# One projection tile, its three kinds of product in another order

## The chip, the cores and the metric

The kernel runs on one core of a Trainium2 chip, as one launch. The metric is the device time of that launch in microseconds (us); the kernel before takes 1693.22 us (median of 3 runs, 1692.78 to 1693.87). Everything is float32 at the interface. The engines that matter here are TensorE (PE in the profile, with its weight loads as PEld), VectorE (DVE) and ScalarE (ACT).

## The reference

Two networks of two layers each, one behind the other. The first prepends 16 meta tokens to 256 tokens, so its activations have 272 columns in the kernel (`T1`); its second layer needs only 256 columns from the out projection on. The second runs on the 256 tokens and, in its first layer, on 256 context tokens beside them (512 columns, `T2`).

```python
# first network, both layers
hn = rms_norm(h, norm_mix_g[l]);  proj = hn @ w_in[l]           # 1024 -> 2560
...                                                             # differential attention, RG-LRU
h = h + jnp.concatenate([o_attn, o_rec], axis=-1) @ w_out[l]    # 1024 -> 1024
hn = rms_norm(h, norm_ffn_g[l])
g, u = jnp.split(hn @ w_gu[l], [D_FF], axis=-1)                 # 1024 -> 2 * 2816
h = h + (jax.nn.silu(g) * u) @ w_down[l]                        # 2816 -> 1024
# second network, both layers: mixer (gmlp and neighbourhood attention, then grouped attention)
f = conv_ffn(modulate(h, ...), w_up[layer], conv_w[layer], conv_b[layer], w_down[layer])
# conv_ffn: h = x @ w_up; 3-tap convolution over tokens; a, g = split; (silu(g) * a) @ w_down
```

Nearly all the arithmetic is in these projections. The down projection takes its input, the hidden rows, from what the up projection before it has just made: that pair occurs in every layer.

## The kernel before, in words

**Precision.** Each float32 operand is held as two parts in a shorter type: a high part and the low rest. A projection is then the sum of three products: high weights by high rows, high weights by low rows, low weights by high rows. Weights arrive by DMA in `raw`. ACT writes the high part to `WH_t` (`split_hi`, L2299, semaphore `w_hi`); DVE subtracts and writes the low part to `WL_t` (`split_lo`, L1572, semaphore `raw_done`, which stands for both parts being there). In the profile both are called `W_t`. The rows are `XH_t`/`XL_t` (normed activations) or, for a down projection, `AH_t`/`AL_t` (hidden rows).

**Tiles.** Weights stay in the array and activations stream. One output tile is 128 output rows by T columns (272, 256 or 512) in one of four banks of `PA`. With a contraction of 1024 there are 8 slices k of 128 and so 24 matmuls; a down projection is done in two halves of the hidden rows, 11 slices and 33 matmuls each. There are thus eight half down projections: two of 272 columns, two of 256, two of 512 and two of 256, in this order of time.

**Order on TensorE.** It is written out by hand. `linear_pe(L)` runs `body(i, s)` for each chunk s of a projection L, and in it each output tile `oo`. Per tile it waits for both parts of the weights (L894), for a free bank, and then goes through the slices. In the first tile of a projection only (`s == 0 and oo == 0`), it also waits, ahead of each slice k, for the rows of that slice: `L.ready(k)`. For normed rows that is `x_ready`, for a down projection it is `hid`, which DVE raises once it has written the low part of hidden slice k (L1618, `hidden_low`). A semaphore is thus raised when both the high and the low rows of a slice are there. Inside a slice the three products follow each other (L917).

**The end of an up projection.** Hidden slice 10 of a half comes from the last pair of up tiles. For the gated kind of the first network ACT and DVE take the two tiles out of PSUM and multiply them; ACT then splits a weight tile (L2299) and writes the high hidden row (L2379), and DVE splits the same weight tile (L1572) and writes the low hidden row (L1618). For the convolving kind of the second network there are the taps (L2457, L1695, L1703), the SiLU (L2469) and the product (L1723) before L2379 and L1618.

**Other paths.** The second tile of a down projection (`second_down`, L953 to L959) and the first four tiles of some projections (`four_tiles`, L977 and L1005) have their own code, which the change leaves alone: they take all products of high weights first, wait for `raw_done`, and then take those of low weights. `out_early` (L872) does half of the first out projection's slices ahead of time. `heads_amid(o, n)` puts a few small matmuls (`spread_heads`, L1449 and L1450, which wait for `m3_rows`) between the slices of two tiles of the last attention's projections; it is called with the slice's number n, at (tile 4, slice 5) and (tile 7, slice 6).

```python
if (o, n) == (4, 5):
    spread_heads(1)
elif (o, n) == (7, 6):
    pe.wait_ge(S("m3_ready"), 2)
    spread_heads(0)
```

Of the kernel before, what the change touches and what calls it, by code (L numbers as in the profile page):

```python
# [24 lines left out]
P = 128  # L25
# [12 lines left out]
RAW = 4  # L38
# [96 lines left out]
def program(nc, hT, ctxT, params, lamv, wgate, wsb, rpb, c_both, c_first, c_second,  # L135
            w_in1, w_out1, w_gu1, w_dn1, w_ada, w_in2, w_out2, w_qkv, w_outc, w_up2, w_dn2, out):
    ctx = ExitStack()
    with ctx:
# [5 lines left out]
        def S(name):  # L144

            if name not in sems:
                sems[name] = ctx.enter_context(nc.semaphore(name))
            return sems[name]
# [8 lines left out]
        WH_t, WL_t = W_t[:, W_at:W_at + 2 * CH], W_t[:, W_at + 2 * CH:W_at + 4 * CH]  # L157
# [195 lines left out]
        def linear(*a, **k):  # L353
            L = Linear(*a, **k)
            if lins:
                lins[-1].next, L.prev = L, lins[-1]
            lins.append(L)
            return L
# [120 lines left out]
        def tiles_ready(n, v=None):  # L479

            v = len(n.groups) - 1 if v is None else v
            return lambda k: ("x_ready", n.value("x_ready", k, v))
# [6 lines left out]
        def norm(writers, *a):  # L489

            n = Norm(*a, alone=not writers, own=0 if not writers else 3 if writers[-1].kt == KD else 1)
            for w in writers:
                w.stat = n
            if writers and isinstance(writers[-1], Linear):
                n.first, n.writer = writers[0], writers[-1]
            plan.append(("norm", n))
            return n

        writers = []
        for l in range(2):  # L500
            n = norm(writers, "pre", l, T1, H1, [(0, T1, ("mixg", l), None)])
# [22 lines left out]
            n = norm([first, rest], "pre", l, T, HV, [(0, T, ("ffng", l), None)])  # L524
# [5 lines left out]
        for l in range(2):  # L530
            both = [(0, SEQ, (l, 0, A_MIX), (0, 0)), (SEQ, T2, (l, 1, A_MIX), (0, 1))]
            T = T2 if l == 0 else SEQ
            if l == 0:
                n = norm(writers, "pre", l, T2, H2, both)
                second_start = n
                rdy = all_ready()
                w = linear("copy", w_in2, 4, T2, XV, None, dst=prj2, held=2, ada=2,
                           parts=[(0, SEQ, tiles_ready(n, 0)), (SEQ, T2, tiles_ready(n, 1))])
# [21 lines left out]
            w = linear("copy", w_out2 if l == 0 else w_outc, 4, T, XV, mixed, dst=YV)  # L560
# [178 lines left out]
        raw_done = [S(f"raw_done{i}") for i in range(RAW)]  # L739

        def repeat(eng, n, step, body, loop=True):

            groups = n // step if loop else 0
            if groups >= 2:
                with eng.Fori(0, groups) as i:
                    for s in range(step):
                        body(i, s)
            else:
                groups = 0
            for s in range(groups * step, n):  # L750
                body(0, s)

        def first(i, s, n):
            return isinstance(i, int) and s < n
# [70 lines left out]
        def _(pe):  # L825
# [14 lines left out]
            def ada_sums(slot, r):  # L840

                b, q = divmod(slot, 4)
                if q == 0:
                    ada_turn()
                    if b:

                        pe.wait_ge(S("ada_free") if b <= 6 else S("ada_row"), b)
                pe.wait_ge(raw_loaded[r % RAW], 16 * (r // RAW + 1))
                for k in (2 * q, 2 * q + 1):
                    for j in range(4):  # L850
                        c = j * 512 + k % 2 * 256
                        mm = pe.matmul(ada_psum[b // 6][0][32 * j:32 * j + 32, :], cpad[:, k, :], RAWV[:, r % RAW, c:c + 256],  # L852
                                       start=(k == 0), stop=(k == 7))
                mm.then_inc(raw_done[r % RAW], 2)
                if q == 3:
                    unturned.append(b)
# [18 lines left out]
            def linear_pe(L):  # L875
                if L.loop:

                    if L.a0:
                        pe.wait_ge(S("of_act"), L.a0)
                    if L.d0:  # L880
                        pe.wait_ge(S("of_dve"), L.d0)
                T, (hi, lo) = L.T, L.rhs

                def body(i, s):
                    for slot, r in L.inline(s):
                        ada_sums(slot, r)
                    if s == 0 and L.after:

                        pe.wait_ge(S(L.after[0]), L.after[1])
                    for oo in range(L.outs):  # L890
                        o = L.outs * s + oo
                        w = L.place(s, oo)

                        pe.wait_ge(raw_done[L.chunk(s, oo)[0] % RAW], L.split(i, s, oo))  # L894
                        if first(i, o, 4):
                            if L.prev and not L.loop and not L.early:

                                name, value = L.prev.evacuated(L.prev.n * L.prev.outs - 4 + o)
                                pe.wait_ge(S(name), value)
                        else:  # L900

                            if L.kind == "copy":
                                pe.wait_ge(S("of_act"), L.a0 + o - 3 + i * (L.outs * L.step))
                            elif L.kind in ("add", "conv"):
                                pe.wait_ge(S("of_dve"), L.d0 + o - 3 + i * (L.outs * L.step))
                            elif oo == 0:
                                pe.wait_ge(S("of_act"), L.a0 + s - 1 + i * L.step)
                            else:
                                pe.wait_ge(S("of_dve"), L.d0 + s - 1 + i * L.step)
                        for n, k in enumerate(L.order):  # L910
                            if s == 0 and oo == 0:

                                name, value = L.ready(k)
                                pe.wait_ge(S(name), value)
                            c = w + k * P
                            for m, (W, X) in enumerate(((WH_t, hi), (WH_t, lo), (WL_t, hi))):
                                mm = pe.matmul(PA[:, (L.b0 + o) % 4, 0:T], W[:, c:c + P], X[:, k, L.x0:L.x0 + T],  # L917
                                               start=(n == 0 and m == 0 and not L.early),
                                               stop=(n == len(L.order) - 1 and m == 2))
                            if L.beside and L.beside[0] == "heads":  # L920
                                heads_amid(L.beside[1] + o, n)
                        mm.then_inc(S("out_ready"), 1)
                        if L.beside:
                            {"gmlp": gmlp_pe, "heads": heads_pe, "first": first_pe}[L.beside[0]](L, L.beside[1] + o)
                    if L.lru and L.lru[1] + s == 3:
                        lru_gates(L.lru[0], 0)

                if L.kt == FH:
                    body(0, 0)
                    second_down(L)  # L930
                    for s in range(2, L.n):
                        body(0, s)
                    return
                if L.parts:
                    four_tiles(L)
                    for s in range(2, L.n):
                        body(0, s)
                    return
                repeat(pe, L.n, L.step, body, L.loop)
# [153 lines left out]
            def lru_gates(l, half):  # L1093

                if half == 0:
                    if l == 0:
                        keep_busy(PB[:, 3, :], 4)

                    pe.wait_ge(S("lr_xs"), l + 1)
                    pe.wait_ge(S("wg_lo"), l + 1)  # L1100
                    if l:

                        pe.wait_ge(S("ada_row"), 3)
                else:

                    pe.wait_ge(S("lr_sg"), 2 * l + 1)
                for i in (2 * half, 2 * half + 1):
                    for g in range(2):
                        w = slice((g * 4 + i) * P, (g * 4 + i + 1) * P)
                        for m, (W, X) in enumerate(((wgh_t, XCH), (wgh_t, XCL), (wgl_t, XCH))):  # L1110
                            mm = pe.matmul(PB[:, i % 2 * 2 + g, 0:T1], W[:, w], X[:, i, :],
                                           start=(m == 0), stop=(m == 2))
                mm.then_inc(S("lr_g"), 1)
# [340 lines left out]
            def heads_amid(o, n):  # L1454
# [8 lines that stand above are left out]
# [1531 lines left out]
```

## Time and profile before

| | |
|---|---|
| median of 3 runs | 1693.22 us (1692.78 to 1693.87) |
| profiled execution, its own time | 1691.35 us |
| its span | 1689.6 us |
| mean granted TensorE clock | 0.994 |
| PE busy | 1616.5 us, 96% |
| PEld busy | 1407.3 us, 83% |
| DVE busy | 1017.9 us, 60% |
| ACT busy | 870.0 us, 51% |
| matmuls, all | 11870 |
| matmuls of L917 | 7800 |

Busy shares say which engine is full on the average; the chain of waits says whose work followed whose up to the end; the timeline gives the start and length of runs of instructions. A matmul's own duration is longer than the distance from its start to the next one's, since they are pipelined: distances between starts are what a matmul costs.

### The profile page before, as it was taken

To read this page: it belongs to the slowest core of one execution; us is meant where nothing else is said; L and a number is where in the kernel's file an instruction comes from. 1 tells how busy PE (TensorE), PEld (TensorE's weight loads), DVE (VectorE), ACT (ScalarE), POOL (GpSimd) and SP (SyncE) were. 2 spreads that over 40 slices of the span, in tenths; PEclk is the share of its full clock that TensorE was granted. 3 is DMA by queue.
4 is the path that set the end of the run, shared out by engine and by line. 5 is a ranking of instruction groups with operands and counts; after the bars stand their busy time and mean duration, and the time that the engine had idled before them with its cause. 6 is when DMAs were issued, how large, how long until landed. Compare 5 with 4: busy or idle time off the path is not lost.

```text
span 1689.6 us, 28191 instructions
## 1 busy us (share of the span) xinstructions
PE 1616.5 (96%) x11870; PEld 1407.3 (83%) x11870; DVE 1017.9 (60%) x1577; ACT 870.0 (51%) x1467; POOL 21.1 (1%) x38
## 2 busy tenths in 40 slices
PE   6999999999999999999989999999999898999997
PEld 6968999989789999987648777888888674789997
DVE  7675545465856555724555764424555777687585
ACT  6764534448545344544564543323444547766563
POOL 0000000000000000300000000000000000000000
PEclk9999999999999999999999999999999999999998
DMA  7465445354556464772202452232213530164642
GB/s 298 145 245 210 160 157 202 135 191 143 200 187 240 152 233 145 220 222 75 75 1 73 177 200 101 86 125 100 84 53 125 200 125 26 52 224 154 233 146 92
DMA packets 60524, 253.94 MB, mean 150 GB/s; under 512 B 4976, under 2 KB 8304, under 8 KB 42480
## 3 DMA queue, kind: packets, MB, share of 16 engines
q1 hardware_dynamic: 59088, 249.01, 41.6%
q0 software_dynamic: 1312, 3.15, 1.0%
q8 instruction: 94, 1.54, 0.4%
q14 instruction: 30, 0.25, 0.0%
HBM read 251.09 MB, written 1.05 MB: 149 GB/s over the span
## 4 chain that ended last, share of the span: by engine, by line
PE 81%; DVE 10%; ACT 6%; issue 2%; DMA 0%; SPq 0%; DVEq 0%; ACTq 0%
PE PA L917 63%; PE PA L977 3%; DVE W_t L1572 2%; PE PB L1340 2%; PE PB L852 2%; PE PA L1005 2%; ACT W_t L2299 1%; PE PB L1327 1%; PE PA L954 1%; PE PA L959 1%; PE PA L953 1%; PE PA L872 1%; PE PB L1270 1%; ACT tmp L2742 1%; PE PA L1412 1%
## 5 line engine op out<-in xcount | busy, mean ns | idle before, releaser
L917 PE MATMUL PA<-XH_t,W_t 128*128 128x256 f32 (+2 forms) x3968 | 873.3, 314 | 4.1 <-DVE W_t L1572 1.8
L917 PEld LDWEIGHTS PA<-XH_t,W_t 128*128 128x128 f32 x3968 | 650.1, 188 | 59.8 <-issue 6.0
L1572 DVE TENSOR_TENSOR W_t<-raw,W_t 128x1024 fp32r<-128x1024 f32 (+1 forms) x344 | 445.0, 1298 | 306.1 <-ACT W_t L2299 305.7
L917 PE MATMUL PA<-XL_t,W_t 128*128 128x256 f32 (+2 forms) x1984 | 620.5, 313 | 0.0
L2299 ACT ACTIVATE W_t<-raw 128x1024 fp32r<-128x1024 f32 (+1 forms) x344 | 381.4, 1113 | 155.6 <-PE PA L917 136.5
L917 PEld LDWEIGHTS PA<-XL_t,W_t 128*128 128x128 f32 x1984 | 373.1, 188 | 23.2 <-issue 0.5
L917 PE MATMUL PA<-AH_t,W_t 128*128 128x256 f32 (+2 forms) x1232 | 266.1, 311 | 0.2
L917 PEld LDWEIGHTS PA<-AH_t,W_t 128*128 128x128 f32 x1232 | 201.2, 188 | 14.1 <-DVE AL_t L1618 0.8
L917 PE MATMUL PA<-AL_t,W_t 128*128 128x256 f32 (+2 forms) x616 | 190.7, 310 | 0.0
L2457 ACT ACTIVATE tmp<-PA,par 128x512 f32<-128x512 f32 (+1 forms) x88 | 58.4, 667 | 133.0 <-PE PA L917 125.3
L1695 DVE SCALAR_TENSOR_TENSOR tmp<-PA,par,tmp 128x510 f32<-128x510 f32 (+1 forms) x88 | 53.6, 613 | 120.5 <-ACT tmp L2457 119.6
L917 PEld LDWEIGHTS PA<-AL_t,W_t 128*128 128x128 f32 x616 | 116.1, 188 | 6.7
L2412 ACT ACTIVATE big<-PA 128x272 f32<-128x272 f32 (+2 forms) x68 | 31.7, 466 | 118.0 <-PE PA L917 107.2
L977 PE MATMUL PA<-XH_t,W_t 128*128 128x256 f32 (+1 forms) x288 | 47.0, 294 | 8.2 <-DVE XL_t L1768 5.1
L2742 ACT ACTIVATE tmp<-PA,small 128x512 f32<-128x512 f32 (+1 forms) x64 | 40.2, 639 | 26.0 <-DVE small L2161 26.0
L2161 DVE TENSOR_REDUCE small<-PA 128x1 f32<-128x512 f32 (+1 forms) x64 | 36.8, 618 | 27.1 <-PE PA L1526 13.0
L852 PE MATMUL PB<-raw,cpad_t 128*32 128x256 f32 x768 | 52.3, 391 | 0.5 <-DMA raw<-in_w_ada 0.4
L977 PEld LDWEIGHTS PA<-XH_t,W_t 128*128 128x128 f32 x288 | 39.5, 193 | 14.8 <-issue 9.6
L1703 DVE SCALAR_TENSOR_TENSOR tmp<-PA,par,tmp 128x510 f32<-128x510 f32 (+1 forms) x88 | 50.1, 608 | 0.3
L1327 PEld LDWEIGHTS PB<-cboth,tmp 128*128 128x128 f32 x224 | 24.2, 140 | 30.7 <-DVE tmp L2170 23.1
L2444 ACT ACTIVATE tmp<-PA 128x272 f32<-128x272 f32 (+1 forms) x44 | 17.1, 390 | 62.2 <-PE PA L917 55.4
L977 PE MATMUL PA<-XL_t,W_t 128*128 128x256 f32 (+1 forms) x288 | 45.1, 289 | 3.1 <-DVE XL_t L1821 3.0
(275 smaller groups left out, 1576.4 us busy)
## 6 DMA issues: line engine op xcount, KB each, us to landing
raw<-in_w_ada SPq DMA_DIRECT2D x48, 1024.0 KB, 5.1
raw<-in_w_gu SPq DMA_DIRECT2D x44, 1024.0 KB, 4.8
raw<-in_w_dn SPq DMA_DIRECT2D x64, 704.0 KB, 4.0
raw<-in_w_up SPq DMA_DIRECT2D x44, 1024.0 KB, 4.8
raw<-in_w_in SPq DMA_DIRECT2D x30, 1024.0 KB, 5.5
raw<-in_w_out SPq DMA_DIRECT2D x12, 1024.0 KB, 4.8
raw<-in_w_qkv SPq DMA_DIRECT2D x6, 1024.0 KB, 6.3
raw<-in_w_outc SPq DMA_DIRECT2D x4, 1024.0 KB, 4.8
```

The lines of the kernel that those rows point to most:

```text
L852: mm = pe.matmul(ada_psum[b // 6][0][32 * j:32 * j + 32, :], cpad[:, k, :], RAWV[:, r % RAW, c:c + 256], start=(k == 0), stop=(k == 7))
L917: mm = pe.matmul(PA[:, (L.b0 + o) % 4, 0:T], W[:, c:c + P], X[:, k, L.x0:L.x0 + T], start=(n == 0 and m == 0 and not L.early), stop=(n == ...
L977: pe.matmul(PA[:, bank % 4, a:b], WH_t[:, c:c + P], x[:, k, a:b], start=(k == 0 and x is hi), stop=False)
L1005: mm = pe.matmul(PA[:, bank % 4, a:b], WL_t[:, c:c + P], hi[:, k, a:b], start=False, stop=(k == KD - 1))
L1327: mm = pe.transpose(PB[:, 2 + c, kb * 128:(kb + 1) * 128], a_P[p % 3][c][:, kb * 128:(kb + 1) * 128], ident)
L1572: dve.tensor_tensor(WL_t[:, w:w + L.cols], RAWV[:, r % RAW, part * UNIT:part * UNIT + L.cols], WHf[:, w:w + L.cols], ALU.subtract).then_in ...
L1695: dve.scalar_tensor_tensor(c[:, :, 1:SEQ], ps[:, :, 0:SEQ - 1], tap(o, 0), c[:, :, 1:SEQ], ALU.mult, ALU.add).then_inc(S("conv_left"), 1)
L1703: dve.scalar_tensor_tensor(c[:, :, 0:SEQ - 1], ps[:, :, 1:SEQ], tap(o, 2), c[:, :, 0:SEQ - 1], ALU.mult, ALU.add).then_inc(S("of_dve"), 1)
L2161: dve.tensor_reduce(a_m[p % 3][:, c:c + 1], PA[:, 2 * (p % 2) + c, 0:width(p)], AX_X, ALU.max, negate=True).then_inc(S(name + "_m"), 1)
L2299: act.activation(WH_t[:, w:w + L.cols], RAWV[:, r % RAW, part * UNIT:part * UNIT + L.cols], ACT.Copy).then_inc(S("w_hi"), 1)
L2457: act.activation(conv[s % 2][x][:, 0:T], PA[:, (L.b0 + o) % 4, 0:T], ACT.Identity, bias=biasv(L.layer)[:, bass.ds(c, 1)], scale=tapv(L.lay ...
L2742: act.activation(a_P[p % 3][c][:, 0:w], PA[:, 2 * (p % 2) + c, 0:w], ACT.Exp, bias=a_m[p % 3][:, c:c + 1], accum_out=a_s[p % 3][:, c:c + 1 ...
```

## The change

Inside a tile the two loops change places. The outer one now goes over the three kinds of product, the inner one over the slices: all high by high, then all high weights by low rows, then all low weights by high rows. At its start a tile waits only for the high weights (`w_hi`); the wait for `raw_done` stands ahead of the third kind. The first tile's waits for its rows stand with the first kind, one per slice. `heads_amid` is called in the second kind.

```diff
-                        pe.wait_ge(raw_done[L.chunk(s, oo)[0] % RAW], L.split(i, s, oo))
+                        pe.wait_ge(S("w_hi"), L.tile(i, s, oo))
                         if first(i, o, 4):
...
-                        for n, k in enumerate(L.order):
-                            if s == 0 and oo == 0:
-
-                                name, value = L.ready(k)
-                                pe.wait_ge(S(name), value)
-                            c = w + k * P
-                            for m, (W, X) in enumerate(((WH_t, hi), (WH_t, lo), (WL_t, hi))):
+                        for m, (W, X) in enumerate(((WH_t, hi), (WH_t, lo), (WL_t, hi))):
+                            if m == 2:
+
+                                pe.wait_ge(raw_done[L.chunk(s, oo)[0] % RAW], L.split(i, s, oo))
+                            for n, k in enumerate(L.order):
+                                if s == 0 and oo == 0 and m == 0:
+
+                                    name, value = L.ready(k)
+                                    pe.wait_ge(S(name), value)
+                                c = w + k * P
                                 mm = pe.matmul(PA[:, (L.b0 + o) % 4, 0:T], W[:, c:c + P], X[:, k, L.x0:L.x0 + T],
                                                start=(n == 0 and m == 0 and not L.early),
                                                stop=(n == len(L.order) - 1 and m == 2))
-                            if L.beside and L.beside[0] == "heads":
-                                heads_amid(L.beside[1] + o, n)
+                                if m == 1 and L.beside and L.beside[0] == "heads":
+                                    heads_amid(L.beside[1] + o, n)
                         mm.then_inc(S("out_ready"), 1)
```

In the changed kernel the matmul of L917 stands on L920, and the lines behind it are three higher.

On TensorE, the first tile of the first half down projection (272 columns), before. L837 are two small matmuls between the up and the down projection; `hid` is the semaphore of the hidden rows, `raw_done1` that of the weights.

```order
L837 MATMUL PB<-cboth,cphase 128x128
L917 MATMUL PA<-AH_t,W_t 128x272 [waits hid,of_act,raw_done1]
L917 MATMUL PA<-AL_t,W_t 128x272
L917 MATMUL PA<-AH_t,W_t 128x272
L917 MATMUL PA<-AH_t,W_t 128x272 [waits hid]
...
L917 MATMUL PA<-AH_t,W_t 128x272 [waits hid]
L917 MATMUL PA<-AL_t,W_t 128x272
L917 MATMUL PA<-AH_t,W_t 128x272
L953 MATMUL PA<-AH_t,W_t 128x272 [waits w_hi,of_dve]
```

The same place in the changed kernel (`x10` is ten such matmuls, each with its own wait):

```order
L837 MATMUL PB<-cboth,cphase 128x128
L920 MATMUL PA<-AH_t,W_t 128x272 [waits hid,of_act,w_hi]
L920 MATMUL PA<-AH_t,W_t 128x272 [waits hid] x10
L920 MATMUL PA<-AL_t,W_t 128x272 x11
L920 MATMUL PA<-AH_t,W_t 128x272 [waits raw_done1]
L920 MATMUL PA<-AH_t,W_t 128x272 x10
L956 MATMUL PA<-AH_t,W_t 128x272 [waits w_hi,of_dve]
```

Before, 30 matmuls of the tile stood ahead of the last wait for `hid` and 2 behind its matmul; now 10 stand ahead and 22 behind.

On TensorE, tile 4 of the last attention's projections (512 columns), with `spread_heads` inside, in the changed kernel:

```order
L920 MATMUL PA<-XH_t,W_t 128x512 [waits x_ready,of_act,w_hi]
L920 MATMUL PA<-XH_t,W_t 128x512 [waits x_ready] x7
L920 MATMUL PA<-XL_t,W_t 128x512 x6
L1452 MATMUL PB<-AL_t,spread 128x256 [waits m3_rows]
L1453 MATMUL PB<-AL_t,spread 128x256
...
L920 MATMUL PA<-XL_t,W_t 128x512 x2
L920 MATMUL PA<-XH_t,W_t 128x512 [waits raw_done0]
L920 MATMUL PA<-XH_t,W_t 128x512 x7
```

The wait for `m3_rows` stood behind 18 matmuls of the tile (six slices of three) and now stands behind 14.

## Rows read from the trace of the kernel before

**Rows 1.** The page's part 1, busy time and share of the span.
```profile
PE 1616.5 (96%) x11870; PEld 1407.3 (83%) x11870; DVE 1017.9 (60%) x1577; ACT 870.0 (51%) x1467; POOL 21.1 (1%) x38
```

**Rows 2.** The page's part 4, the chain of waits.
```profile
PE 81%; DVE 10%; ACT 6%; issue 2%; DMA 0%; SPq 0%; DVEq 0%; ACTq 0%
PE PA L917 63%; PE PA L977 3%; DVE W_t L1572 2%; PE PB L1340 2%; PE PB L852 2%; PE PA L1005 2%; ACT W_t L2299 1%; PE PB L1327 1%; PE PA L954 1%; PE PA L959 1%; PE PA L953 1%; PE PA L872 1%; PE PB L1270 1%; ACT tmp L2742 1%; PE PA L1412 1%
```

**Rows 3.** L917's idle time by releaser: us, times; whole span, 1345 to 1360, 1495 to 1520.
```profile
DVE W_t L1572: 5.4, 10
...
DVE W_t L1572: 2.9, 4
...
DVE W_t L1572: 2.1, 5
```

**Rows 4.** Timeline of PE, 512 columns: start, us, engine, line, operands, count.
```profile
1075.97 0.39 PE L917 MATMUL PA<-AH_t,W_t 128*128 128x512 f32 x1
1083.36 0.39 PE L917 MATMUL PA<-AH_t,W_t 128*128 128x512 f32 x1
...
1271.35 2.70 PE L959 MATMUL PA<-AH_t,W_t 128*128 128x512 f32 x11
1273.89 0.39 PE L917 MATMUL PA<-AH_t,W_t 128*128 128x512 f32 x1
```

**Rows 5.** Timeline, PE, ACT and DVE, around the third half down projection (256 columns).
```profile
572.96 0.36 PE L917 MATMUL PA<-AH_t,W_t 128*128 128x256 f32 x1
576.87 0.28 PE L917 MATMUL PA<-AH_t,W_t 128*128 128x256 f32 x1
...
573.02 1.38 ACT L2299 ACTIVATE W_t<-raw 128x1408 fp32r<-128x1408 f32 x1 [2.39 <-PE PA L917]
...
574.50 1.63 DVE L1572 TENSOR_TENSOR W_t<-raw,W_t 128x1408 fp32r<-128x1408 f32 x1 [0.99 <-ACT W_t L2299]
576.05 0.42 DVE L1618 TENSOR_TENSOR AL_t<-tmp,AH_t 128x256 fp32r<-128x256 f32 x1
```

**Rows 6.** Timeline, PE and DVE, end of the eighth one's first tile (256 columns).
```profile
1649.85 0.39 PE L917 MATMUL PA<-AH_t,W_t 128*128 128x256 f32 x1
1650.07 0.28 PE L917 MATMUL PA<-AL_t,W_t 128*128 128x256 f32 x1
...
1649.36 0.43 DVE L1618 TENSOR_TENSOR AL_t<-tmp,AH_t 128x256 fp32r<-128x256 f32 x1 [0.49 <-ACT AH_t L2379]
```

**Rows 7.** Timeline, PE and DVE, the first one's first tile (272 columns).
```profile
227.82 0.37 PE L917 MATMUL PA<-AH_t,W_t 128*128 128x272 f32 x1
231.93 0.29 PE L917 MATMUL PA<-AH_t,W_t 128*128 128x272 f32 x1
...
230.91 0.43 DVE L1618 TENSOR_TENSOR AL_t<-tmp,AH_t 128x272 fp32r<-128x272 f32 x1
```

**Rows 8.** Timeline, DVE, the fifth half down projection (512 columns).
```profile
1081.14 0.69 DVE L1618 TENSOR_TENSOR AL_t<-tmp,AH_t 128x512 fp32r<-128x512 f32 x1 [0.70 <-ACT AH_t L2379]
```

**Rows 9.** Timeline, PE and DVE, first tile of the second in projection (272 columns).
```profile
371.80 0.41 PE L917 MATMUL PA<-XH_t,W_t 128*128 128x272 f32 x2
...
370.20 1.14 DVE L1768 TENSOR_TENSOR XL_t<-tmp,XH_t 128x272 fp32r<-128x272 f32 x3
```

**Rows 10.** Timeline, PE and DVE, first tile of the first out projection.
```profile
137.15 0.39 PE L917 MATMUL PA<-XH_t,W_t 128*128 128x272 f32 x1
...
136.68 1.02 DVE L2097 TENSOR_TENSOR XL_t<-big,XH_t 128x272 fp32r<-128x272 f32 x2
```

**Rows 11.** Timeline, PE, `spread_heads` inside tile 4 of the last attention's projections.
```profile
1370.00 0.39 PE L1449 MATMUL PB<-AL_t,spread 32*128 32x256 f32 x2 [0.56 <-DVE AL_t L2216]
```

**Rows 12.** Timeline, PE, the matmuls behind the tiles between 1345 and 1360.
```profile
1359.78 1.96 PE L1429 MATMUL PB<-big,cphase 128*128 128x256 f32 x8 [0.49 <-DVE XL_t L1821]
```

**Rows 13.** Windows: stretch, length, busy of PE, PEld, DVE, ACT, POOL; PEclk, DMA, GB/s.
```profile
458.70:465.40 6.70, 6.70 (x36) 3.97 (x35) 3.07 (x14) 2.38 (x11) 0.00 (x0) 0.50 0.24 89
```

**Rows 14.** Waits of PE: waiting line, releaser: us in total, times, longest us.
```profile
PE PB L1327 <- ACT big L2754: 11.8, 11, 1.8
```

## The prediction

> **What bounds the kernel now.** I read the busy shares first: TensorE is busy for 96% of the span, DVE for 60% and ACT for 51% [rows 1]. The chain of waits agrees: 81% of the span is PE's, and L917, the line the change rewrites, holds 63% [rows 2]. So whatever delays TensorE by a microsecond costs about one, and whatever only helps ACT or DVE costs or gives nothing. Then I asked what L917 itself waits for: of all its idle time only 5.4 us, in 10 places, end with DVE's low weights [rows 3]. That is all that the new, earlier start of a tile can win. It leaves two questions: does the order of the products change what one costs, and which of the moved waits is not yet met at its new place?
>
> **The cost of one product.** At 512 columns the old order takes 32 steps from the first to the last product of a tile, 1083.36 - 1075.97 = 7.39 us, or 0.231 us a step; a run of 11 low-weight products in the new manner takes 1273.89 - 1271.35 = 2.54 us, again 0.231 us [rows 4]. At 272 columns a step in the old order is (231.93 - 227.82 - 0.09) / 32 = 0.126 us [rows 7], at 256 (576.87 - 572.96 - 0.10) / 32 = 0.119 us [rows 5]; what is taken off is the restart explained below. The number of matmuls, weight loads, ACT and DVE instructions does not change, nor any DMA. So the steady state costs the same, term 0, by rows that show either order.
>
> **Down projections, the main term.** The first tile needs hidden slice 10, which DVE finishes long after the tile's start. In the third half down projection the tile starts at 572.96 and L1618 ends at 576.05 + 0.42 = 576.47, 3.51 us later [rows 5]. Nothing in the tile causes that time: ACT waits for the last up tile, splits weights for 1.38 us and writes the high row, DVE splits for 1.63 us, then writes the low row [rows 5]. Before, 30 products (30 x 0.119 = 3.6 us) stood ahead of that wait and just covered it; now 10 do (1.2 us), and TensorE stands still for about 2.3 us. It is late next by what lies behind: the product that needed the row, and 22 more steps. The trace gives both small numbers. In the eighth, L1618 ends at 1649.36 + 0.43 = 1649.79 and its matmul starts at 1649.85, 0.06 us later; the next starts at 1650.07, 0.22 us on instead of 0.12, a restart of 0.10 us [rows 6]. So the new start of the last product is (end of L1618) + 0.06 + 0.10 + 22 steps:
> - 256 columns: 576.47 + 0.16 + 2.62 = 579.25 against 576.87: 2.38 us. There are four such places.
> - 272 columns: L1618 ends at 231.34; 231.34 + 0.16 + 2.77 = 234.27 against 231.93: 2.34 us [rows 7]. Two places.
> - 512 columns: L1618 ends at 1081.14 + 0.69 = 1081.83 [rows 8]; 1081.83 + 0.16 + 5.08 = 1087.07 against 1083.36 [rows 4]: 3.71 us. Two places.
>
> Together 4 x 2.38 + 2 x 2.34 + 2 x 3.71 = 21.6 us. Behind the waiting matmul stands all of TensorE's queue, the second down tile first; what ACT and DVE hold then waits for that tile's end, so nothing of theirs comes sooner. Slice 9 is no trouble: it is one pair of up tiles older.
>
> **Other first tiles.** The in projection of the second layer starts while its normed rows still come in. The last three low rows are written by 370.20 + 1.14 = 371.34, and the tile's last product started at 371.80 [rows 9]. The new order has 16 products behind the last row's: 371.34 + 0.16 + 16 x 0.126 = 373.52, 1.7 us later. In the out projection of the first layer the fourth row is there at 136.68 + 1.02 = 137.70; its product now stands fourth, at 137.15 + 0.10 + 0.38 = 137.63, instead of tenth [rows 10]: 0.13 + 0.10 = 0.2 us. Two more such tiles (the other out projections with rows still coming) look alike, so 0.7 us for three. All other first tiles find their rows ready.
>
> **Small matmuls inside a tile.** `spread_heads` in tile 4 already waited for DVE's row until 1370.00 [rows 11]. It now comes 18 - 14 = 4 products earlier, waits the longer for it and leaves four more behind: 4 x 0.231 = 0.9 us. In tile 7 it moves by six products; the trace before shows no wait there at all, so I take nothing, with 6 x 0.231 = 1.4 us as the other end.
>
> **What is won.** Of the 5.4 us, 2.9 lie between 1345 and 1360 [rows 3]. There the next matmul, L1429, waits for a DVE row until 1359.78 whatever TensorE did before [rows 12], so they are given back: bounds 0 and 2.9, I take 0. Another 2.1 us lie between 1495 and 1520 [rows 3]. DVE only starts on a low part once ACT's high part is there, and that step takes it over a microsecond (1.63 us for the larger tile in rows 5), so with the high part alone these tiles start sooner; TensorE then runs ahead of DVE and may meet it again. I take 1.5 of the 2.1; bounds 0 and 2.1.
>
> **The sum** is 21.6 + 1.7 + 0.7 + 0.9 - 1.5 = 23.4 us. The profiled execution took 1691.35 us and would take 1714.7. The median of the runs, 1693.22, is 1.9 us above that execution: 1716.6 us, 1.4% slower. A difference under 0.2% (3.4 us) could not be told from none.
>
> **A cost with wide bounds: the clock.** TensorE's granted clock stood at 0.50 of full speed, its lower level of 1.2 GHz, for 6.7 us in a stretch in which matmuls were sparse (x36) [rows 13]. In the two 512-column places there will now be 1081.89 - (1075.97 + 0.10 + 9 x 0.231) = 3.7 us from one start to the next. Outside the start-up, the longest wait of TensorE for another engine before is 1.8 us [rows 14], so a gap of that length is not shown, and the cost lies between 0 and half of 6.7 us for each of the two places; at 256 and 272 columns the distance is 2.4 us, nearer to the 1.8 us. I take 0 for all. The Trainium skill, page "TensorE: Matmul & The Clock Gate", section "HAM oscillation — how this bites in real kernels", speaks against this change: gaps in which TensorE idles send the clock back to half, and the matmuls behind them pay. By that rule the sum would be higher by what the first rival below gives; the trace agrees that the clock falls to 0.50 when little is issued, and does not show that one gap is enough.
>
> **The rivals.**
> - The clock falls behind the two long gaps. For it: rows 13. Against it: the tiles on both sides of a gap are dense. Half speed over 6.7 us loses half of that, 3.35 us, once or twice: 1720.0 to 1723.3 us.
> - Part of the gaps is paid back. Later waits of TensorE that something else than TensorE sets (low weights, rows that DVE writes) shrink by the delay. For it: L917's 5.4 us and other lines' waits. Against it: in the tails of stages ACT and DVE start from TensorE's last tile and move with it. About 5 us: 1711.6 us.
> - The order changes the step. High weights stood twice in a row before and no longer do. Against it: the equal 0.231 us in both orders [rows 4]. There are 7800 products on L917, so 1 ns each way is 7.8 us: 1708.8 or 1724.4 us.
> - Not slower: the earlier start wins and the moved wait costs nothing. It would need hidden slice 10 within 10 steps of the tile's start, 1.2 us at 256 columns; from there on the gap is zero. Then the price is at most what L917 waits for low weights, 5.4 us: 1687.8 us. Against it stand 3.51 us in rows 5, of which 1.38 and 1.63 us are weight splits that the change doesn't touch.
>
> **How the numbers follow.** My forecast 0.60 (1713.5 to 1719), the clock 0.21, paid back 0.08, another step 0.08, not slower 0.03. The range of 1709 to 1723 us leaves out the last case and the edges of two more. Slower by over 0.2%: 0.95; within 0.2%: 0.03; faster: 0.02.
>
> **What would show it.** In the profile after, the first tile of each down projection has an idle time before L920 of about 2.1 us (3.3 at 512 columns, where the longer matmul is taken off) ended by DVE's `AL_t` L1621, eight times; the waits for `W_t` at L920 fall to 1 us or less; the distance between products stays at 0.12, 0.126 and 0.231 us; L1452 waits 1.5 us once; the in projection of the second layer ends its first tile 1.7 us later. I am wrong if these gaps are there and the span is still not some 23 us longer (then something pays back), if the granted clock shows 0.50 near the 512-column gaps, or if hidden slice 10 comes earlier than 3.5 us after the up projection's last tile.

## The result and the profile after

The changed kernel takes 1727.9 us (median of 4 runs, 1718.0 to 1730.94) against 1693.0 us for the kernel before in the same comparison (4 runs, 1692.76 to 1693.87). The ratio is 1.0191, interval 1.0166 to 1.0216: 1.9% slower (the two medians alone give 1.0206). The forecast was 1716.6 us with a range up to 1723. The direction is right, and the size is short by 11.3 us, which is a third of the loss of 34.9 us. On the chips of the experiments below, 31 runs of the kernel before took 1690.07 to 1697.41 us; one more, at a granted clock of 0.579, took 2564.09 us and is in no ratio.

The profiled execution took 1730.94 us (span 1729.2, granted clock 0.983) against 1691.35 (span 1689.6, granted clock 0.994). In the profile after, the rewritten matmul line is L920, and what was L1572, L1618, L1768, L1821, L1429 and L959 is L1575, L1621, L1771, L1824, L1432 and L962.

Its page, part 1, busy time and share of the span:

```profile
PE 1634.8 (95%) x11870; PEld 1423.9 (82%) x11870; DVE 1018.4 (59%) x1577; ACT 870.1 (50%) x1467; POOL 21.0 (1%) x38
```

The counts are those of [rows 1]. TensorE's busy time has grown by 18.3 us with the same 11870 matmuls, so some of them run slower. The chain (part 4) keeps the shape of [rows 2], PE 81% and the rewritten line 63%, and tells nothing of this.

What TensorE waits for (waiting line, releaser: us in total, times, longest us):

```profile
PE PA L920 <- DVE AL_t L1621: 20.7, 8, 3.4
PE PB L1330 <- ACT big L2757: 11.8, 11, 1.8
...
PE PB L1432 <- DVE XL_t L1824: 2.3, 1, 2.3
```

A new first row has come in: eight waits for the low hidden row, 20.7 us. The row that led before stands below it unchanged [rows 14]. No row of L920 for `W_t` is left; the same view of the kernel before had one:

```profile
PE PA L917 <- DVE W_t L1572: 1.8, 3, 0.7
```

The 5.4 us of [rows 3] are another count: that view adds the idle time ahead of weight loads (3.6 us) to that ahead of matmuls (1.8 us). The third row above is a wait that has taken the place of what was won (below).

Four of the eight gaps, the first, second, third and fifth (272, 272, 256 and 512 columns), in the timeline of PE (start, us, engine, line, operands, count, idle before and its releaser), and behind the second the products that follow:

```profile
232.84 0.48 PE L920 MATMUL PA<-AH_t,W_t 128*128 128x272 f32 x1 [2.08 <-DVE AL_t L1621]
...
336.64 0.39 PE L920 MATMUL PA<-AH_t,W_t 128*128 128x272 f32 x1 [2.30 <-DVE AL_t L1621]
336.87 1.54 PE L920 MATMUL PA<-AL_t,W_t 128*128 128x272 f32 x11
338.25 1.54 PE L920 MATMUL PA<-AH_t,W_t 128*128 128x272 f32 x11
...
587.69 0.39 PE L920 MATMUL PA<-AH_t,W_t 128*128 128x256 f32 x1 [2.14 <-DVE AL_t L1621]
...
1100.85 0.79 PE L920 MATMUL PA<-AH_t,W_t 128*128 128x512 f32 x1 [3.43 <-DVE AL_t L1621]
```

and what ends two of them, in the timeline of DVE:

```profile
587.21 0.42 DVE L1621 TENSOR_TENSOR AL_t<-tmp,AH_t 128x256 fp32r<-128x256 f32 x1
...
1100.11 0.69 DVE L1621 TENSOR_TENSOR AL_t<-tmp,AH_t 128x512 fp32r<-128x512 f32 x1 [0.69 <-ACT AH_t L2382]
```

587.21 + 0.42 + 0.06 = 587.69: the restart follows DVE's low row by the 0.06 us read from [rows 6]. The idle times are 2.08, 2.30, 2.14, 2.37, 3.43, 3.42, 2.37 and 2.57 us: as forecast (about 2.1, and 3.3 at 512 columns) or a little longer. The second place is also as forecast behind the gap: 336.87 to 338.25 is 11 steps of 0.126 us. At the others the next products are slower. Windows ahead of and behind a gap (stretch, length, busy time and count of PE, PEld, DVE, ACT, POOL, granted clock PEclk, DMA share, GB/s):

```profile
232.90:236.40 3.50, 3.50 (x16) 3.50 (x17) 0.00 (x0) 0.00 (x0) 0.00 (x0) 0.51 0.57 206
...
333.50:336.60 3.10, 0.84 (x7) 0.62 (x5) 2.11 (x3) 2.81 (x4) 0.00 (x0) 1.00 0.02 7
336.70:340.10 3.40, 3.40 (x27) 3.40 (x28) 0.27 (x1) 0.27 (x1) 0.00 (x0) 1.00 0.60 210
...
584.50:588.00 3.50, 1.36 (x11) 1.16 (x11) 2.14 (x3) 1.45 (x3) 0.00 (x0) 1.00 0.13 53
588.00:591.40 3.40, 3.40 (x18) 3.40 (x17) 0.00 (x0) 0.00 (x0) 0.00 (x0) 0.50 0.60 212
...
1096.60:1100.00 3.40, 0.82 (x4) 0.34 (x2) 2.12 (x4) 1.78 (x3) 0.00 (x0) 1.00 0.00 0
1100.00:1106.80 6.80, 5.95 (x14) 4.69 (x15) 2.23 (x2) 0.07 (x1) 0.00 (x0) 0.50 0.30 106
```

Read the rows in pairs. PE is wholly busy behind the first and third gap and yet does 16 and 18 matmuls where the same length behind the second holds 27: the clock is at half, 1.2 GHz. A step takes 0.227 us instead of 0.126 (272 columns), 0.213 instead of 0.117 (256) and 0.427 instead of 0.231 (512). The trace before has two half-speed stretches after the first microseconds and ahead of the last ones, around 110 and 460 us ([rows 13] is the second). The trace after has twelve. Seven begin at one of the eight gaps (all but the second): five last 3.4 us and two, at 1100.0 and 1683.7, last 6.8 us.

The table has, for each first tile of a half down projection, the time from the first to the last product, in us, before and after, and how the difference splits. "Wait" is worked out as in the prediction, from the end of DVE's row at that place in the profile after; "clock" is the rest, and stands where the clock fell.

| place | columns | before | after | more | forecast | wait | clock |
|---|---|---|---|---|---|---|---|
| 1 | 272 | 4.11 | 7.97 | 3.85 | 2.34 | 2.3 | 1.5 |
| 2 | 272 | 4.07 | 6.59 | 2.52 | 2.34 | 2.5 | no fall |
| 3 | 256 | 3.91 | 7.78 | 3.87 | 2.38 | 2.4 | 1.5 |
| 4 | 256 | 4.04 | 7.86 | 3.82 | 2.38 | 2.4 | 1.4 |
| 5 | 512 | 7.39 | 13.81 | 6.43 | 3.71 | 3.7 | 2.7 |
| 6 | 512 | 7.38 | 12.66 | 5.28 | 3.71 | 3.7 | 1.6 |
| 7 | 256 | 4.15 | 8.02 | 3.88 | 2.38 | 2.4 | 1.5 |
| 8 | 256 | 4.26 | 8.79 | 4.53 | 2.38 | 2.4 | 2.1 |

With 0.6 us more in the tile behind place 8, these are 34.8 of the 39.6 us between the two profiled executions: 21.8 us of waits and 13.0 us of clock. The rest: 3.2 us in the in projection of the second layer, 1.4 us ahead of the first down projection, 0.9 us from 1345 to 1403 (times of the trace before), 1.2 us won from there to the seventh down projection, and some 0.5 us in pieces.

The spread of the four runs goes with the clock too. Their times and granted clocks are 1730.94 (0.983), 1718.0 (0.991), 1730.19 (0.984) and 1725.61 (0.986). Taking off (1 - clock) x span leaves 1701.5, 1702.6, 1702.5 and 1701.5 us. The kernel before leaves 1691.35 - 0.006 x 1689.6 = 1681.2 by the same sum. So by this sum waits and order cost about 21 us in every run, and the clock adds between some 5 us (0.991) and some 19 us (0.983). Both are estimates: the clock's last digit is good to 0.9 us, and the sum counts time at half clock in which TensorE waited anyway. Place by place, the profiled execution has some 16 us of clock in it and not 19.

### The profile page after: what moved, and what is told of

It is laid out like the page before. It is cut to its first block, busy times and chain, and to the rows that moved or that the text cites. A ratio compares the mean times of both kernels' runs of the same rounds, so it can differ in the third digit from the quotient of the medians.

```text
span 1729.2 us, 28191 instructions
## 1 busy us (share of the span) xinstructions
PE 1634.8 (95%) x11870; PEld 1423.9 (82%) x11870; DVE 1018.4 (59%) x1577; ACT 870.1 (50%) x1467; POOL 21.0 (1%) x38
## 4 chain that ended last, share of the span: by engine, by line
PE 81%; DVE 10%; ACT 6%; issue 2%; DMA 0%; SPq 0%; DVEq 0%; ACTq 0%
PE PA L920 63%; PE PA L980 3%; DVE W_t L1575 2%; PE PA L1008 2%; PE PB L1343 2%; PE PB L852 1%; ACT W_t L2302 1%; PE PB L1330 1%; PE PA L956 1%; PE PA L957 1%; PE PA L962 1%; PE PA L872 1%; PE PB L1273 1%; ACT tmp L2745 1%; DVE Y L1957 1%
## 5 line engine op out<-in xcount | busy, mean ns | idle before, releaser
L920 PE MATMUL PA<-XH_t,W_t 128*128 128x256 f32 (+2 forms) x3968 | 653.5, 315 | 3.4 <-DVE XL_t L1771 2.4
L1575 DVE TENSOR_TENSOR W_t<-raw,W_t 128x1024 fp32r<-128x1024 f32 (+1 forms) x344 | 445.1, 1299 | 324.3 <-ACT W_t L2302 323.8
L920 PEld LDWEIGHTS PA<-XH_t,W_t 128*128 128x128 f32 x3968 | 566.3, 188 | 58.5 <-issue 6.5
L920 PE MATMUL PA<-XL_t,W_t 128*128 128x256 f32 (+2 forms) x1984 | 340.9, 313 | 0.0
L920 PEld LDWEIGHTS PA<-XL_t,W_t 128*128 128x128 f32 x1984 | 288.5, 188 | 23.4
L920 PE MATMUL PA<-AH_t,W_t 128*128 128x256 f32 (+2 forms) x1232 | 200.2, 315 | 20.7 <-DVE AL_t L1621 20.7
L920 PEld LDWEIGHTS PA<-AH_t,W_t 128*128 128x128 f32 x1232 | 177.0, 193 | 36.3 <-DVE AL_t L1621 22.8
L920 PE MATMUL PA<-AL_t,W_t 128*128 128x256 f32 (+2 forms) x616 | 109.2, 329 | 0.0
L920 PEld LDWEIGHTS PA<-AL_t,W_t 128*128 128x128 f32 x616 | 94.9, 204 | 7.4
L980 PEld LDWEIGHTS PA<-XH_t,W_t 128*128 128x128 f32 x288 | 40.2, 197 | 15.7 <-issue 9.7
```

Source lines behind the costliest of these rows:

```text
L980: pe.matmul(PA[:, bank % 4, a:b], WH_t[:, c:c + P], x[:, k, a:b], start=(k == 0 and x is hi), stop=False)
L1575: dve.tensor_tensor(WL_t[:, w:w + L.cols], RAWV[:, r % RAW, part * UNIT:part * UNIT + L.cols], WHf[:, w:w + L.cols], ALU.subtract).then_in ...
```

## The experiments

Theory A: the whole loss comes from hidden slice 10, whose wait now has 23 products behind it, and the gap that this opens also brings the clock down. Rivals, by the letters that the expectations use: the new order itself is slower in all tiles (B); the clock's falls have nothing to do with the gaps (C). A third, without a number in the expectations, is that the other first tiles or the small matmuls take a large part (D). All kernels are the changed one with the tile body made into a list of steps (kind m of product, slice n), so that a first tile can have another list than the rest. "slices" is the order of before, "kinds" that of the change:

```python
slices = [(m, n) for n in range(N) for m in range(3)]
kinds  = [(m, n) for m in range(3) for n in range(N)]
pairs  = [(m, n) for n in range(N) for m in range(2)] + [(2, n) for n in range(N)]
held   = [(m, n) for m in range(3) for n in range(N - 1)] + [(m, N - 1) for m in range(3)]
```

`is_first` is `s == 0 and oo == 0`, and `down` is `L.kt == FH`. All ratios are against the kernel before on the same chip.

### e1, e2, e3: which tiles carry the loss

```diff
-mode = "kinds"
+mode = "slices" if is_first and down else "kinds"      # e1
+mode = "slices" if is_first else "kinds"               # e2
+mode = "kinds" if is_first and down else "slices"      # e3
```

> The change, with the old order (slice by slice) put back in the first tile of each of the eight half down projections only. Theory A (the moved wait for the hidden rows costs 21.6 us, and the clock that falls behind its gaps some 14 us more): about 1697 us, the gaps before the hidden rows gone and the clock at half speed in fewer stretches, with the in projection of the second layer still 1.7 us late. Rival B (the grouped order or the wait inside every tile costs in all tiles): above 1715 us. Rival C (the waits cost 21.6 us, but the clock's falls have nothing to do with them): about 1709 us.

> The change only in tiles that are not the first of a projection; all first tiles in the old order. Theory A: what is left is the gain of starting on the high weights, 0 to 2 us: 1691 to 1693 us, clock as in the kernel before. Rival B: above 1715 us. Rival C: about 1705 us, with the clock's falls still there.

> The reverse of the first: only the first tile of each half down projection is grouped by kind, all other tiles as before. Theory A: 1693 + 21.6 + some 14 of clock, 1723 to 1730 us. Rival B: 1693 to 1696 us. Rival C: about 1715 us.

Measured: e1 1697.31 us, ratio 1.0022 (1.0012 to 1.0033; ten runs from 1692.61 to 1699.74). e2 1692.65 us, ratio 0.9994 (0.9983 to 1.0006). e3 1723.72 us, ratio 1.0182 (1.0166 to 1.0197).

e3 has the old order everywhere but in eight tiles of 33 products, and has nearly all of the change's 1.0191. e1, its complement, has 0.22%: that is the other first tiles (1.7 + 0.7 us forecast), the small matmuls and three clock falls, at 161, 373 and 1455 us, less what is won. e2 keeps the new order in every tile but the first ones and cannot be told from before. B falls, and D is worth about 4 us. C had asked for 1709 us of e1 and 1715 us of e3.

e3's waits of PE:

```profile
PE PA L936 <- DVE AL_t L1636: 20.7, 8, 3.4
PE PA L936 <- DVE W_t L1590: 1.8, 3, 0.7
```

The first is the changed kernel's row to the tenth; the second is the old order's wait for low weights, as before. In this execution the clock fell behind five of the eight gaps. Windows of e3, around the first place (no fall) and behind the third and fifth:

```profile
228.00:231.90 3.90, 1.83 (x16) 1.61 (x14) 2.42 (x3) 1.77 (x3) 0.00 (x0) 1.00 0.19 79
231.90:235.00 3.10, 3.10 (x24) 3.10 (x25) 0.00 (x0) 0.00 (x0) 0.00 (x0) 1.00 0.65 229
...
582.80:586.10 3.30, 3.30 (x18) 3.30 (x17) 0.03 (x1) 0.03 (x1) 0.00 (x0) 0.50 0.47 184
...
1094.80:1101.40 6.60, 5.66 (x13) 4.45 (x14) 2.23 (x2) 0.16 (x1) 0.00 (x0) 0.50 0.31 109
```

The first place has the same gap as in the changed kernel and keeps its full clock here. Whether a 2-us gap brings the clock down is thus not the same from one execution to another.

### e4, e8: the same waits, with TensorE kept busy

Filler matmuls on constants stand ahead of slice 10's wait, in a bank of `PA` that the next tile starts afresh, once that bank's old content has been taken out; they are issued by `keep_busy` (L862), which the kernel has already. If A is right the waits stay, and the falls go.

```diff
+if is_first and down and x == 10:
+    name, value = L.prev.evacuated(L.prev.n * L.prev.outs - 3)
+    pe.wait_ge(S(name), value)
+    keep_busy(PA[:, (L.b0 + 1) % 4, :], 8 if T < T2 else 14)     # e4; e8: 4 and 7
```

> The change in full, and in each first down tile, ahead of the wait for the last hidden slice, 8 matmuls whose result nobody reads (14 at 512 columns), so that TensorE is not idle in the gap. They take about 1.7 us (3.0 us) of gaps of 2.3 us (3.6 us). Theory A: the waits stay, the clock no longer falls behind them: about 1716 us, and a narrower spread of the runs. Rival C: no less than the change itself, 1725 us or more. If the waiting itself were not the cost but something TensorE does then, no change either.

Measured for e4: 1728.57 us, ratio 1.0215 (1.0198 to 1.0232). The expectation missed. The timeline of PE at the third place says why:

```profile
583.75 1.10 PE L940 MATMUL PA<-AH_t,W_t 128*128 128x256 f32 x8
584.69 3.62 PE L862 MATMUL PA<-cboth 128*128 128x256 f32 x16
587.95 0.47 PE L940 MATMUL PA<-AH_t,W_t 128*128 128x256 f32 x1
```

Eight fillers show as 16 matmuls: a float32 filler is two passes of 0.216 us here, so eight last 3.45 us, longer than the gap they were to fill. The clock did not fall behind any of the eight places, but the fillers' own length replaced it. e8 halves their number.

> The run before this one with fillers was spoilt by their length: one such matmul is two passes of 0.216 us, so 8 took 3.45 us and pushed the waited-for product back by about 1.1 us (2.4 us at 512 columns), some 12 us in all. Here 4 fillers (7 at 512 columns), 1.7 us (3.0 us), shorter than the gap. Theory A: the waits cost 23.4 us as before, the clock falls only in the in projection of the second layer and the norm stages, as it did with the down tiles in the old order: 1717 to 1719 us. Rival C (the falls have nothing to do with the gaps): 1725 us or more.

Measured for e8: 1718.58 us, ratio 1.0151 (1.0134 to 1.0167), as expected. Its PE timeline, waits, and windows over the third and fifth gap:

```profile
582.28 1.89 PE L862 MATMUL PA<-cboth 128*128 128x256 f32 x8
```

```profile
PE PA L940 <- DVE AL_t L1640: 4.3, 8, 0.9
```

```profile
584.00:587.50 3.50, 3.08 (x26) 2.91 (x25) 0.53 (x2) 0.00 (x0) 0.00 (x0) 1.00 0.58 198
...
1094.00:1100.00 6.00, 5.59 (x25) 4.31 (x24) 2.21 (x2) 0.00 (x0) 0.00 (x0) 1.00 0.36 121
```

The fillers take up most of each gap, the clock stands at 1.00 behind all eight, and the places take 2.34, 2.52, 2.33, 2.34, 3.71, 3.71, 2.38 and 2.37 us more than before: 21.7 us, where the prediction had 21.6. Against the kernel before on their own chips, the filled gap is 0.4% better than the empty one (1.0151 and 1.0191; the intervals just touch). It speaks against C: in the two profiled executions with filled gaps, e4 and e8, the clock fell at none of 16 places, against 7 of 8 and 5 of 8 with empty ones. The four runs of e8 lie within 1.04 us.

### e5, e7, e6: how many products stand ahead of the wait

The old order has 30 products ahead of slice 10's wait, the change 10. e5 has 20, e7 none (its list is that of before, but it waits for slice 10 at the tile's start). e6 has 30 again, though in the manner of the change: all products of slices 0 to 9 by kind, then the three of slice 10.

```diff
+mode = ("pairs" if down else "slices") if is_first else "kinds"   # e5
+mode = ("held"  if down else "slices") if is_first else "kinds"   # e6
+if is_first and down: pe.wait_ge(*hidden slice 10)  # e7, ahead of the first product; else as e2
```

> First down tiles in the order of the second ones: high and low rows by high weights slice by slice, then all low weights. 20 products ahead of the last hidden slice's, 12 behind the waiting one. All other first tiles in the old order, the rest grouped by kind. Theory A (only what stands behind the wait counts): the last product starts at the end of the low hidden row + 0.16 us + 12 steps, 1.2 us later than before at 256 columns, 1.1 at 272, 1.4 at 512: 9.7 us in all, gaps of about 1 us, no fall of the clock: 1702 us. Rival B (grouping by kind is what costs): half way of the change or more, 1710 us.

> First down tiles in the old order, but the wait for the last hidden slice stands ahead of the whole tile: 0 products ahead, 32 behind the waiting one. The rest as in the kernel with all first tiles in the old order. Theory A: 3.6 us each at 256 and 272 columns, 6.0 at 512, 33.5 us in all, and the clock falls behind all eight gaps (3.5 and 5.9 us long), some 15 us: 1740 us; without the clock's part 1726 us. Rival B: 1693 us.

> First down tiles grouped by kind over slices 0 to 9, and the three products of slice 10 last: the wait stands behind 30 products as before the change. All other first tiles in the old order, the rest grouped. Theory A: 1692 to 1694 us, no gap over 0.3 us. Rival B: 1710 us or more.

Measured: e5 1703.16 us, ratio 1.0063 (1.0046 to 1.0080). e7 1744.61 us, ratio 1.0312 (1.0283 to 1.0340). e6 1694.32 us, ratio 1.0000 (0.9989 to 1.0012). e6 lies 0.3 us above its range by the median and level with before by the ratio; e7 is 4.6 us above its 1740 us, in a profiled execution whose clock fell for 6.8 us and not 3.4 at several of the gaps.

The waits of PE for the low hidden row in e5, e7 and e6:

```profile
PE PA L936 <- DVE AL_t L1636: 8.9, 8, 1.4
```

```profile
PE PA L939 <- DVE AL_t L1639: 34.1, 8, 5.9
```

```profile
PE PA L936 <- DVE AL_t L1636: 0.2, 1, 0.2
```

With 30, 20, 10 and 0 products ahead, the eight waits add up to 0.2, 8.9, 20.7 and 34.1 us. In e5 the places cost 1.08, 1.26, 1.17, 1.17, 1.40, 1.41, 1.17 and 1.21 us, together 9.9 us (9.7 expected), and the clock fell at none. In e7 it fell at all eight. Windows of e7, of the fifth place's gap and behind it:

```profile
1102.00:1105.80 3.80, 0.00 (x0) 0.00 (x0) 2.41 (x5) 2.03 (x3) 0.00 (x0) 1.00 0.00 0
1106.00:1112.60 6.60, 5.97 (x14) 4.75 (x15) 1.91 (x2) 0.00 (x0) 0.00 (x0) 0.50 0.33 109
```

So with gaps of at most 1.4 us the clock fell in 0 of 8 places, with the change's gaps in 7 of 8 and 5 of 8 (the changed kernel and e3), and with the longest in 8 of 8. e6 shows that the manner doesn't matter: every place lies within 0.02 us of before. In these tiles the loss is set by how many products wait behind the last row, and by the clock that the gap brings down.

e2 and e6 are faster than the changed kernel by nearly 2%, and level with the kernel before. None of the versions beat that one.

## Why the prediction was right and where it failed

**The down projections.** Right, mechanism and size. The eight places cost 21.7 us where only the wait is at work (e8), against 21.6, and the doses of e5 and e7 follow the same sum. e3 puts the loss there and e2 clears the rest.

**The steady state.** Right: the steps are 0.117, 0.126 and 0.231 us at full clock (the 0.119 of the prediction holds a second small delay of its tile), and e2 is at 0.9994.

**The clock. This is the step that failed.** "I take 0 for all" was said of all eight gaps. The rule of the Trainium skill quoted there pointed to a real cost; what I made of it was a rival for the two 512-column places alone, since the 2.4 us of the others lay near the 1.8 us of [rows 14], which left no trace on the clock. The term was put at 0 and measured 13.0 us. In the profiled execution five of the seven falls at these gaps are at 256 or 272 columns. The seven cost 13.0 us together: 1.4 to 1.6 us each where the fall lasted 3.4 us, and 2.7 us where it lasted 6.8 us. The Trainium skill, page "TensorE: Matmul & The Clock Gate", section "HAM oscillation — how this bites in real kernels", would have the matmuls behind idle gaps pay at half rate, and by that rule the trace agrees: 18 matmuls in 3.4 us where 29 fit at 0.117 us a step. e8 shows that the gap is the cause: filled, it costs the wait alone.

[rows 13] were misread besides. In that stretch, and in the one ahead of it, TensorE was busy throughout, with small matmuls (24 of those between 455.5 and 459.9 us have 16 columns); the one ahead is

```profile
455.30:458.70 3.40, 3.40 (x27) 3.12 (x27) 2.54 (x14) 2.11 (x8) 0.00 (x0) 0.99 1.01 355
```

So outside its start-up the kernel before showed neither a fall behind a gap nor a gap longer than 1.8 us without one. The 0 rested on 2.4 us being near 1.8 us, and for the two places at 3.7 us on no row.

**The other first tiles.** The wait of the second in projection was 1.7 us, by the sum of the prediction with DVE's rows of the profile after. Here too the clock then fell. Timeline of PE, changed kernel:

```profile
378.49 1.09 PE L920 MATMUL PA<-XH_t,W_t 128*128 128x272 f32 x3 [0.37 <-DVE XL_t L1771]
...
380.93 3.17 PE L920 MATMUL PA<-XH_t,W_t 128*128 128x272 f32 x16
```

Windows of it, ahead of the fall and in it:

```profile
376.40:379.70 3.30, 2.18 (x9) 1.25 (x9) 3.30 (x9) 1.29 (x3) 0.00 (x0) 1.00 0.00 0
379.90:383.10 3.20, 3.20 (x16) 3.20 (x16) 0.37 (x1) 0.11 (x1) 0.00 (x0) 0.50 0.57 156
```

With the clock the place cost 3.2 us and not 1.7, with no idle time of PE longer than a part of a microsecond in these rows: nine products dripped in as DVE wrote the rows. In all four traces with the new order in this tile (the changed kernel, e1, e4 and e8) the clock fell here, and in none of the five experiments with the old order. Of the 0.7 us for the out projections, the first one's 0.2 is there: in the same four traces TensorE is 0.2 us later behind that tile than ahead of it. The fall at 161.3 us, still ahead of the first down projection, cost 1.5 us more.

**What is won.** From 1345 to 1360 I took 0 of the 2.9 us, as L1432 would wait for a DVE row anyway. It did, and worse. PE's timeline and windows:

```profile
1390.45 3.49 PE L1432 MATMUL PB<-big,cphase 128*128 128x256 f32 x8 [2.33 <-DVE XL_t L1824]
```

```profile
1386.70:1390.10 3.40, 1.42 (x12) 1.17 (x10) 1.77 (x3) 3.40 (x9) 0.00 (x0) 1.00 0.14 60
1390.20:1393.50 3.30, 3.05 (x7) 2.52 (x8) 3.30 (x4) 2.90 (x4) 0.00 (x0) 0.50 0.81 281
```

The tiles ahead ended 1.85 us sooner, and the wait grew from the 0.49 us of [rows 12] to 2.33: all of it was given back. In this execution the clock fell behind the longer gap, and the 8 matmuls took 3.49 us instead of 1.96. The gap of 2.2 to 2.3 us is in eight traces, and the clock fell at it in three (the changed kernel, e5 and e8).

Between 1495 and 1520 some 1.45 us were won (1.5 forecast). That the forecast was met owes something to luck. The 2.1 us that it was a part of are the weight loads' idle time (1.5 us) and the matmuls' (0.5 us) added up, and so are the 2.9 and the 5.4 us; no row of the prediction gives the 1.5.

**The small matmuls.** The +0.9 us were met. In the profiled execution the wait of L1452 can't be seen, since the half clock behind L1432 had just used it up. In e1, where the clock did not fall there, PE's timeline has it (1.5 forecast):

```profile
1374.10 0.39 PE L1467 MATMUL PB<-AL_t,spread 32*128 32x256 f32 x2 [1.44 <-DVE AL_t L2234]
```

From 1345 to 1403 of the trace before, TensorE falls back by 0.9 us in each of the four kernels with the moved call (the changed kernel, e1, e4 and e8), whether the clock fell there or not, and by less than 0.1 us in e2, e6 and e7, which have the old order in this tile. So the 1.5 us of clock at L1432 cost nothing here in the end: they went into a wait for DVE's row that would have come anyway.

**Why the median is off by 11.3 us.** In the profiled execution the terms add up: waits 21.8, second in projection 1.7, first out projection 0.2, small matmuls 0.9, won 1.45, which is 23.2 us against 23.4 forecast, and on top some 16 us of clock, of which 13.0 at the gaps. The median after holds, by the estimate above, 21 us or a little more of waits and order, and up to 14 us of clock, against 0. The fastest run, 1718.0 us at a clock of 0.991, lies 1.4 us above the forecast; by its clock it had few falls, but no trace of it was kept. The clock rival's 1723.3 us was the edge of the range, and the cost passed it since it came in most of eight places and not in two.

**What stays open.** What decides in one execution whether a 2-us gap brings the clock down. Nor are gaps needed: the stretch ahead of the fall at 161.3 us has none of the new waits, reads alike in both kernels, and only one fell. Windows after, then before:

```profile
157.90:161.30 3.40, 1.77 (x26) 1.01 (x27) 3.00 (x6) 1.58 (x5) 0.00 (x0) 1.00 1.00 348
161.30:164.70 3.40, 3.40 (x17) 3.40 (x17) 3.40 (x10) 2.09 (x5) 0.00 (x0) 0.50 0.95 393
```

```profile
157.90:161.30 3.40, 1.71 (x25) 0.94 (x26) 2.95 (x7) 1.60 (x4) 0.00 (x0) 1.00 0.97 345
161.30:164.70 3.40, 3.40 (x28) 3.40 (x28) 3.40 (x10) 2.14 (x5) 0.00 (x0) 1.00 0.95 400
```

The same work gives 17 matmuls in one and 28 in the other. That this is a matter of when the stretch falls is a guess that no run here tested.

## What to carry to other kernels

The cost of a wait inside an in-order queue is set by what stands ahead of it until the data come and by what is left behind it: put the products of the slice that arrives last at the end, all of them, and the order of the rest is free (e6). Price a new gap on TensorE with the clock behind it, as a range that changes from run to run, and not with the idle time alone. Before adding up idle times, see whether a view counts a matmul and its weight load apart. Where runs of one kernel spread by more than those of another, set the granted clock beside each time before explaining anything else.

## What the runs showed that was not expected

- Gaps of 2.1 to 2.6 us, in the middle of dense projections, brought TensorE to half clock in 5 of 6 such places of one execution (the changed kernel) and in 3 of 6 of another (e3); for gaps of at most 1.4 us (e5) it was none of 8.
- The changed kernel's time varies with the granted clock, 1718.0 to 1730.94 us in four runs, against 1692.76 to 1693.87 for the kernel before beside it. The gaps alone don't make the spread: e3 has all eight, and its four runs lie between 1721.34 and 1724.11 us.
- Half clock costs nothing while TensorE would wait for another engine anyway: 1.5 us lost behind L1432 were gone again at the next wait.
- A float32 filler matmul of 256 columns is two passes of 0.216 us, while a product of the projections takes one step of 0.117 us.
- A gap filled with useless products that end before it does was no dearer, and by the medians cheaper, than an empty one: 1718.58 us against 1727.9 (not side by side; the ratios against the kernel before are 1.0151 and 1.0191). With twice the filler (e4) it was 1728.57 us.
